# Attention values of all four head pairs projected in one token-major series ahead of the pair loop

## The chip, the cores and the metric

One core of a Trainium2 chip. The metric is the device time of one execution in microseconds (us), as the median of several runs.

## What is computed

Two transformer-like blocks over 512 tokens of width 1024, all in float32. The change touches the first block's attention: `z = rms_norm(x) @ w_in` is split into q, k, v (512 columns each, 8 heads of 64) and zu, zv (512 each, for a gating branch).

```python
q, k, v, zu, zv = jnp.split(z, [D_ATTN, 2*D_ATTN, 3*D_ATTN, 3*D_ATTN + D_SGU], axis=-1)
q = q.reshape(B, S, N_ATTN_HEADS, HEAD_DIM) * (HEAD_DIM ** -0.5)
attn = dilated_attention(q, k, v, rel_bias)
sgu = spatial_gating(jax.nn.gelu(zu), jax.nn.gelu(zv), sgu_ln_g, sgu_ln_b, sgu_w, sgu_b)
mix = jnp.concatenate([attn, sgu], axis=-1) @ w_out
```

The rest (output projection, feed-forward, and a second block of convolution, pooling, a recurrence and gated feed-forwards) is the same in both kernels.

## The kernel before, in words

Activations lie channel-major: partitions are channels, the free axis is the 512 tokens. Each float32 factor is split into a high and a low part; a product of two is three matmuls (low weights x high activations, high x low, high x high) added in PSUM. Weights come in *units* of two tiles of 128x512: SyncE loads `raw` (a ring of `RING` = 4 units), ScalarE rounds it to `whi` (`split`, two units ahead of use), GpSimd makes `wlo = raw - whi` (`lo_parts`), and TensorE waits for `unit_lo`. `unit_begun` counts units that TensorE has begun, and frees ring slots for `split`. PSUM has 8 banks of 128x512; `bank_plan` writes out by hand which stage uses which bank, and the counters `filled` and `drained` hand them over. Every engine has its own program, in the order in which the code is written.

The start: x is transposed and normalised; the zv projection goes by tokens (`unit_by_tokens`: the activations are the stationary operand, so the result has tokens on partitions) into banks 0 to 3. Then TensorE transposes the convolution taps and the eight gate weights (`small`), and projects pair 0 (`group(U_QKV, 0, "qkv0", up_tags)`): 4 units, 96 matmuls, into bank 0 (q), 1 (k), 2 (v), 3 (u = zu). A unit holds two k-tiles of the columns of all four outputs of one pair. Then come the gate's mixes and the pair loop. `PAIRS` = 4, two heads each.

`attend(p)` on TensorE: the value product of the pair before (`values`, L2221), the transposes of this pair's values (`values_turned`, L2212), and then eight weight tiles i, each a score product (`scores`, L2204 and L2205, bank 4 or 5), a bias and maximum on VectorE (`biased`), an exponential on ScalarE (`weights`, L1280), a scaling on VectorE (`scaled_weights`, L2919 and L2922) and four transposes (`turn`, L2240, bank 6 or 7) that ScalarE copies out (`turned`, L1286). Between them stand pieces of the next pair's projection (`dense`, L2000), cut by a table; one piece is three matmuls:

```python
def attend(p, piece, before_it, following=None,
           cuts=(0, 2, 4, 6, 8, 10, 12, 14, 16, 18, 20, 22, 24, 28, 30, 31, 32)):
```

The last pair has pieces of the output projection instead, under its own table `(0, 2, 4, 5, 7, 8, 10, 11, 13, 14, 15, 16, 17, 20, 21, 24)`. Scores 0 and 1 of the next pair come at the end of a pair; they need q and k as high parts (`drain_head`, ScalarE) and low parts (`qk_low`, VectorE). ScalarE also copies v out of bank 2 (`drain_values`) and the turned values into `vtok` (`values_copied`). Pairs 1 and 2 are a hardware loop on TensorE and ScalarE, pairs 0 and 3 are written out. VectorE's program is written out for all.

Of the kernel before, what the change touches and what calls it, by code (L numbers as in the profile page):

```python
# [23 lines left out]
P = 128  # L24
SEQ = 512
# [47 lines left out]
U_QKV = U_ZV + 4  # L73
U_WOUT = U_QKV + 4 * PAIRS
# [161 lines left out]
def bank_plan():  # L236
# [43 lines left out]
def build(nc, x, w, vec, sgu_w, sgu_b, rel_bias, dw_w, pool_w, ident_c, onehot_c, lnmult_c,  # L280
# [4 lines left out]
    with ExitStack() as ctx:  # L285
# [35 lines left out]
        with ExitStack() as s:  # L321
            first_table = sb("first_table", [P, PHASES * SHIFTS, P], scope=s)
            below_pdiff = sb("below_pdiff", [P, 12 * SEQ - PHASES * SHIFTS * P], scope=s)
            pdiff = sb("pdiff", [P, 4, SEQ], scope=s)
        m_hi = sb("m_hi", [P, KT, SEQ], F32R)
# [9 lines left out]
        with ExitStack() as s:  # L335
# [10 lines left out]
            vT = rs  # L346
# [9 lines left out]
            vtok = sb("vtok", [P, SEQ], scope=s)  # L356

# [258 lines left out]

        def own_rows(e):

            return slice(HEAD_DIM * e, HEAD_DIM * (e + 1))
# [103 lines left out]
        def _(sp):  # L723
# [45 lines left out]
            qkv(0, (0, 1))  # L769
# [9 lines left out]
            qkv(0, (2, 3))  # L779
# [6 lines left out]
            for p in range(1, PAIRS):  # L786
                qkv(p, range(4))
                bias_table(p)
# [326 lines left out]
        def _(act):  # L1115
# [124 lines left out]
            split(U_QKV, 0)  # L1240
# [4 lines left out]
            split(U_QKV, 1)  # L1245
# [17 lines left out]
            def drain_values(stage, turn):  # L1263
                act.wait_ge(filled[2], nth(stage, ("m", 2), turn))
                act.activation(vT[:, :], bank(stage, ("m", 2)), ACT.Copy).then_inc(drained[2], 1)

            drain_head("qkv0", 0, 0, 0)
            drain_head("qkv0", 0, 0, 1)
            drain_values("qkv0", 0)
            split(U_QKV, 3)  # L1270
# [5 lines left out]
            def attend(p, u_count, units, before_it, following=None):  # L1276
# [12 lines left out]
                def values_copied():  # L1289
                    act.wait_ge(filled[6], nth("att", "vtok", p))  # L1290
                    act.activation(vtok[:, :], bank("att", "vtok"), ACT.Copy).then_inc(drained[6], 1)

# [14 lines left out]
                if following is None:  # L1307
                    weights(1)
                    values_copied()
# [21 lines left out]
                values_copied()  # L1331
# [20 lines left out]
                units(3)  # L1352
# [4 lines left out]
                drain_values("qkv", following)  # L1357

            u_first = nth("qkv0", ("m", 3))
            attend(0, u_first, lambda i: split(U_QKV + 4, i), None, 0)  # L1360
            with act.Fori(0, PAIRS - 2) as r:
                attend(r + 1, r + (u_first + 1), lambda i: split(U_QKV + 8, i, r, 4), r, r + 1)
# [617 lines left out]
        def _(pe):  # L1980
# [184 lines left out]
            for j in range(1, 4):  # L2165
                unit_by_tokens(j)

            pe.wait_ge(small_in, 16 * 2)
            pe.wait_ge(drained[5], before("small", "taps"))
            pe.transpose(bank("small", "taps")[:, 0:4 * TAPS], trows[:, :], ident[0:4 * TAPS, 0:4 * TAPS])\  # L2170
                .then_inc(filled[5], 1)
            for i in range(2):
                pe.wait_ge(drained[4 + i], before("small", f"ws{i}"))
                for g in range(4):
                    mm = pe.transpose(ps[:, 4 + i, g * P:(g + 1) * P], wsin[:, 4 * i + g, :], ident[:, :])
                mm.then_inc(filled[4 + i], 1)

            group(U_QKV, 0, "qkv0", up_tags)
# [28 lines left out]
            def values_turned(p):  # L2207

                pe.wait_ge(drained[2], nth("qkv0", ("m", 2)) + p)
                pe.wait_ge(drained[6], before("att", "vtok", p))  # L2210
                for t in range(TT):
                    mm = pe.transpose(ps[:, 6, t * P:(t + 1) * P], vT[:, t * P:(t + 1) * P], ident[:, :])  # L2212
                mm.then_inc(filled[6], 1)

            def values(p):

                pe.wait_ge(drained[6], nth("att", ("t", 6), p))
                pe.wait_ge(drained[7], before("att", "o", p))
                for k in range(TT):
                    for e in range(2):  # L2220
                        mm = pe.matmul(ps[own_rows(e), 7, :], vtok[:, k * P + HEAD_DIM * e:k * P + HEAD_DIM * (e + 1)],  # L2221
                                       probT[:, e, k, :], start=k == 0, stop=k == TT - 1)
                mm.then_inc(filled[7], 1)

            def attend(p, piece, before_it, following=None,
                       cuts=(0, 2, 4, 6, 8, 10, 12, 14, 16, 18, 20, 22, 24, 28, 30, 31, 32)):

                def dense(n):
                    lo, hi = cuts[n], cuts[n + 1]
                    for j in range(4):  # L2230
# [14 lines left out]
                values_turned(p)  # L2245
# [16 lines left out]

            def head_units(j0, j, part, turn=0, per=0):
                behind_mixes = j0 == 4 and j == 0
                unit(U_QKV + j0, j, h_hi, h_lo, (2 * j, 2 * j + 1), "qkv", up_tags, j == 0, j == 3, turn, per,
                     (2, 0, 1, 3) if behind_mixes else (0, 1, 2, 3), use=turn + (j0 // 4 - 1), part=part)
# [21 lines left out]
            attend(0, lambda j, part: head_units(4, j, part), None, 1)  # L2288
            with pe.Fori(0, PAIRS - 2) as r:
                attend(r + 1, lambda j, part: head_units(8, j, part, r, 4), r, r + 2)  # L2290
# [387 lines left out]
        def _(dve):  # L2678
# [153 lines left out]
            for b in (5, 6):  # L2832
# [3 lines left out]
            dve.wait_ge(filled[5], nth("small", "taps"))  # L2836
            dve.tensor_copy(taps[:, 0:TAPS, :], bank("small", "taps")[:, 0:4 * TAPS].rearrange("p (t j) -> p t j", j=4))\
                .then_inc(drained[5], 1)
            for i in range(2):
                dve.wait_ge(filled[4 + i], nth("small", f"ws{i}"))  # L2840
                dve.tensor_copy(wsT[:, 4 * i:4 * i + 4, :], bank("small", f"ws{i}").rearrange("p (g t) -> p g t", t=P))\
                    .then_inc(drained[4 + i], 1)


# [9 lines left out]
            for t in range(TT):  # L2854
                dve.wait_ge(drained[t], nth("zv", ("t", t)))
                dve.tensor_scalar(zneg[:, t:t + 1], zsum[:, t:t + 1], -1.0 / (4 * P), None, ALU.mult).then_inc(zmean_ready, 1)
            for e in range(2):
# [1117 lines left out]
```

## Time and profile before

| | us |
|---|---|
| median of 3 runs | 1688.95 (1688.62 to 1689.82) |
| the profiled execution | 1689.87 |
| its span, first to last instruction | 1687.8 |
| TensorE busy in it | 1679.1 |
| VectorE, ScalarE, GpSimd busy | 1242.8, 810.6, 424.0 |

The span is what the rows lie in; the execution's time is 2.1 us more. A busy TensorE is not TensorE at its peak, since matmul ends are modelled; the start times of its rows are what to compute with.

### The profile page before, as it was taken

Reading aid. Unit: us, or ns where it says so; the run is one execution under the profiler, and the core shown is the slowest. Engines: PE = TensorE matmul, PEld = TensorE weight load, DVE = VectorE, ACT = ScalarE, POOL = GpSimd, SP = SyncE. Lnnn points to the kernel's source line nnn. Section 1 sums busy time; section 2 is a strip of 40 time slices with the busy share of each in tenths; the row PEclk is TensorE's granted clock in tenths of the full one; section 3 lists DMA queues with packets and bytes.
Section 4 is the critical chain, followed back from the end, with each engine's and each line's share of the span. In section 5 each row is a group of like instructions: output and inputs, shape, how many; then the busy total and the mean of one; then the engine's idle time right before and its main releaser. Section 6 shows DMA issues by size and latency. Waiting matters only on the chain.

```text
span 1687.8 us, 29256 instructions
## 1 busy us (share of the span) xinstructions
PE 1679.1 (99%) x9774; PEld 1468.6 (87%) x9774; DVE 1242.8 (74%) x2276; ACT 810.6 (48%) x1429; POOL 424.0 (25%) x217
## 2 busy tenths in 40 slices
PE   9999999999999999999999999999999999999998
PEld 7877788999998888889999998888888889999997
DVE  5656579888887878688688686576675598688685
ACT  5566563333332534754353354565655554343354
POOL 3332320000001497320220213432523310220221
PEclk9999999999999999999999999999999999999999
DMA  7542223333333233233332333231222233332331
GB/s 210 123 107 79 75 74 101 95 106 100 99 99 99 81 114 104 72 100 108 105 120 81 102 109 101 82 94 50 87 62 76 65 112 111 101 124 75 100 113 50
DMA packets 160146, 163.16 MB, mean 97 GB/s; under 512 B 10659, under 2 KB 126999, under 8 KB 160063
## 3 DMA queue, kind: packets, MB, share of 16 engines
q1 hardware_dynamic: 155599, 159.19, 31.1%
q10 hardware_dynamic: 4464, 2.89, 0.6%
q8 instruction: 49, 0.80, 0.2%
q14 instruction: 34, 0.28, 0.1%
HBM read 158.36 MB, written 3.67 MB: 96 GB/s over the span
## 4 chain that ended last, share of the span: by engine, by line
PE 93%; POOL 3%; DVE 1%; issue 1%; ACT 0%; DMA 0%; SPq 0%; DVEq 0%; POOLq 0%; ACTq 0%
PE ps L2000 36%; PE ps L2459 21%; PE ps L2484 10%; PE ps L2338 7%; PE ps L2363 6%; PE ps L2028 2%; PE ps L2566 1%; POOL wlo L1002 1%; PE ps L2039 1%; PE ps L2221 1%; PE ps L2240 1%; POOL wsum L1045 1%; POOL first_table L1008 0%; DMA lnmult<-const_lnmult 0%; PE ps L2204 0%
## 5 line engine op out<-in xcount | busy, mean ns | idle before, releaser
L1002 POOL TENSOR_TENSOR wlo<-raw,whi 128x1024 fp32r<-128x1024 f32 x60 | 145.2, 2436 | 588.4 <-ACT whi L1489 292.6
L2000 PE MATMUL ps<-h_hi,wlo 128*128 128x512 f32 x608 | 247.4, 407 | 0.1
L2000 PE MATMUL ps<-h_hi,whi 128*128 128x512 f32 x608 | 237.8, 391 | 0.0
L2000 PE MATMUL ps<-h_lo,whi 128*128 128x512 f32 x608 | 237.6, 391 | 0.0
L1124 ACT ACTIVATE whi<-raw 128x1024 fp32r<-128x1024 f32 x120 | 124.5, 1053 | 115.2 <-PE ps L2000 101.2
L2000 PE MATMUL ps<-m_hi,wlo 128*128 128x512 f32 x384 | 152.7, 398 | 0.3 <-POOL m_lo L1066 0.3
L2000 PE MATMUL ps<-m_hi,whi 128*128 128x512 f32 x384 | 149.7, 390 | 0.0
L2000 PE MATMUL ps<-m_lo,whi 128*128 128x512 f32 x384 | 149.7, 390 | 0.0
L2000 PEld LDWEIGHTS ps<-h_hi,whi 128*128 128x128 f32 x608 | 114.1, 188 | 25.3
L2000 PEld LDWEIGHTS ps<-h_hi,wlo 128*128 128x128 f32 x608 | 114.4, 188 | 22.2 <-issue 0.8
L2000 PEld LDWEIGHTS ps<-h_lo,whi 128*128 128x128 f32 x608 | 114.5, 188 | 20.9 <-issue 0.5
L1081 POOL TENSOR_TENSOR wlo<-raw,whi 128x512 fp32r<-128x512 f32 x30 | 43.1, 1467 | 355.3 <-ACT whi L1697 355.3
L3597 DVE TENSOR_TENSOR xT<-xT,ps 128x512 f32<-128x512 f32 x95 | 64.8, 686 | 86.1 <-PE ps L2484 56.6
L995 POOL TENSOR_TENSOR wlo<-raw,whi 128x1024 fp32r<-128x1024 f32 x36 | 87.7, 2442 | 160.9 <-ACT whi L1124 144.8
L1689 ACT ACTIVATE whi<-wsums 128x512 fp32r<-128x512 f32 x88 | 53.4, 626 | 147.9 <-DVE wsums L3465 147.9
L1102 POOL TENSOR_TENSOR wlo<-raw,whi 128x1024 fp32r<-128x1024 f32 x28 | 68.2, 2466 | 129.3 <-ACT whi L1124 129.3
L2459 PE MATMUL ps<-h_hi,wlo 128*128 128x256 f32 x352 | 99.6, 283 | 0.0
L2459 PE MATMUL ps<-h_lo,whi 128*128 128x256 f32 x352 | 99.6, 283 | 0.0
L2459 PE MATMUL ps<-h_hi,whi 128*128 128x256 f32 x352 | 99.6, 283 | 0.0
L2000 PEld LDWEIGHTS ps<-m_hi,wlo 128*128 128x128 f32 x384 | 72.1, 188 | 16.2 <-issue 1.5
L2000 PEld LDWEIGHTS ps<-m_hi,whi 128*128 128x128 f32 x384 | 72.1, 188 | 15.3
L2000 PEld LDWEIGHTS ps<-m_lo,whi 128*128 128x128 f32 x384 | 72.2, 188 | 14.8 <-issue 0.7
(506 smaller groups left out, 4931.6 us busy)
## 6 DMA issues: line engine op xcount, KB each, us to landing
raw<-in_ffn_w SPq DMA_DIRECT2D x264, 256.0 KB, 2.9
raw<-in_w_ff SPq DMA_DIRECT2D x128, 256.0 KB, 2.9
raw<-in_hg_w_in SPq DMA_DIRECT2D x64, 256.0 KB, 3.1
raw<-in_w_in SPq DMA_DIRECT2D x40, 256.0 KB, 4.8
raw<-in_cp_w_in SPq DMA_DIRECT2D x24, 256.0 KB, 2.9
raw<-in_w_out SPq DMA_DIRECT2D x16, 256.0 KB, 2.9
raw<-in_cp_w_out SPq DMA_DIRECT2D x16, 256.0 KB, 2.8
raw<-in_hg_w_out SPq DMA_DIRECT2D x16, 256.0 KB, 2.7
```

What stands on the lines that cost most here:

```text
L995: pool.tensor_tensor(wlo[:, u % RING, :, :], raw[:, u % RING, :, :], whi[:, u % RING, :, :].bitcast(F32), ALU.subtract).then_inc(unit_lo, 1)
L1002: pool.tensor_tensor(wlo[:, u % RING, :, :], raw[:, u % RING, :, :], whi[:, u % RING, :, :].bitcast(F32), ALU.subtract).then_inc(unit_lo, 1)
L1081: pool.tensor_tensor(lo_slot(s), raw[:, u % RING, d % 2, :], hi_slot(s).bitcast(F32), ALU.subtract)\
L1102: pool.tensor_tensor(wlo[:, u % RING, :, :], raw[:, u % RING, :, :], whi[:, u % RING, :, :].bitcast(F32), ALU.subtract).then_inc(unit_lo, 1)
L1124: act.activation(whi[:, u % RING, :, :], raw[:, u % RING, :, :], ACT.Copy).then_inc(unit_hi, 1)
L1689: act.activation(in_tiles(hi_slot(form_slot(layer, n))), form_source(layer, j, f), ACT.Copy)\
L2000: mm = pe.matmul(ps[:, b, :], wt[:, s, a, m * P:(m + 1) * P], xt[:, kts[a], :], start=starts and a == 0 and i == 0, stop=last)
L2338: mm = pe.matmul(ps[:, b, 0:HALF], wt[:, k * P:(k + 1) * P], xt[:, k, :], start=begins and TAGS[f] != "c11", stop=ends, skip_group_check=T ...
L2363: mm = pe.matmul(ps[:, 4 + m, :], wt[:, m * P:(m + 1) * P], xt[:, kt, :], start=kt == 0 and r == 0, stop=last)
L2459: mm = pe.matmul(ps[:, b, 0:HALF], wt[:, k * P:(k + 1) * P], xt[:, k, :], start=begins and TAGS[f] != "c11", stop=ends, skip_group_check=T ...
L2484: mm = pe.matmul(ps[:, 4 + m, :], wt[:, m * P:(m + 1) * P], xt[:, kt, :], start=kt == 0 and r == 0, stop=last)
L3597: dve.tensor_tensor(xT[:, k, :], xT[:, k, :], ps[:, 4 + m, :], ALU.add).then_inc(drained[4 + m], 1)
```

## The change

A new stage `v` of four units projects the values of all pairs ahead of pair 0, by tokens as zv is: the result is `vtok[:, p, ...]` with tokens on partitions, in banks 4 to 7, and ScalarE copies each bank out once. A pair's projection is then three units, one per output tile in the order k, q, u (`QKV_TILES = (1, 0, 3)`), each with all eight k-tiles of 128 columns. The transposes of the values, `vT`, `drain_values` and `values_copied` go. The taps and gate weights are transposed between the value units. The cuts table is shortened to 24 pieces, and pairs 1 and 2 are written out on TensorE and ScalarE.

```diff
-U_QKV = U_ZV + 4
-U_WOUT = U_QKV + 4 * PAIRS
+U_V = U_ZV + 4
+U_QKV = U_V + 4
+U_WOUT = U_QKV + 3 * PAIRS
+QKV_TILES = (1, 0, 3)
...
-    b.stage("small", [("taps", 5), ("ws0", 4), ("ws1", 5)])
-    b.stage("qkv0", up)
-    b.stage("sgu", [(("mix", j), (6, 7, 0, 1)[j]) for j in range(4)])
-    b.stage("qkv", up, PAIRS - 1)
-    b.stage("att", [("vtok", 6)] + [(("s", i), 4 + i % 2) for i in range(8)]
+    b.stage("small", [("taps", 2), ("ws0", 3), ("ws1", 2)])
+    b.stage("v", [(("t", t), 4 + t) for t in range(TT)])
+    b.stage("qkv0", [(("m", m), m) for m in QKV_TILES])
+    b.stage("sgu", [(("mix", j), (6, 7, 2, 0)[j]) for j in range(4)])
+    b.stage("qkv", [(("m", m), m) for m in QKV_TILES], PAIRS - 1)
+    b.stage("att", [(("s", i), 4 + i % 2) for i in range(8)]
...
-            def qkv(p, tiles):
-                for j in tiles:
-                    load(U_QKV, j, [wi[:, 2 * j + a, 0:4, p * P:(p + 1) * P] for a in range(2)], p, 4)
+            def v(units):
+                for j in units:
+                    load(U_V, j, [wi[:, 2 * j + a, 2, :] for a in range(2)])
+
+            def qkv(p):
+                for j, m in enumerate(QKV_TILES):
+                    load(U_QKV + 3 * p, j, [wi[:, 4 * a:4 * a + 4, m, p * P:(p + 1) * P] for a in range(2)])
...
             bias_table(0)
-            for p in range(1, PAIRS):
-                qkv(p, range(4))
-                bias_table(p)
+            for p in range(PAIRS):
+                qkv(p)
+                if p:
+                    bias_table(p)
...
+            split(U_V, 2)
+            act.preload_act_table_set(EXP_TABLES)
+            split(U_V, 3)
+            split(U_QKV, 0)
+            for t in range(TT):
+                act.wait_ge(filled[4 + t], nth("v", ("t", t)))
+                act.activation(vtok[:, :, t * P:(t + 1) * P], in_tiles(bank("v", ("t", t))), ACT.Copy)\
+                    .then_inc(drained[4 + t], 1)
+            split(U_QKV, 1)
             split(U_QKV, 2)
-            act.preload_act_table_set(EXP_TABLES)
...
+            def value_unit(j):
+
+                s = (U_V + j) % RING
+                pe.wait_ge(unit_lo, U_V + j + 1)
+                for a in range(2):
+                    k = 2 * j + a
+                    for i, (xt, wt) in enumerate(((h_hi, whi), (h_lo, whi), (h_hi, wlo))):
...
+                        for t in range(TT):
...
+                            mm = pe.matmul(ps[:, 4 + t, :], xt[:, k, t * P:(t + 1) * P], wt[:, s, a, :], start=begins, stop=ends)
...
+            def head_unit(p, j, part=slice(0, 8)):
+
+                stage, turn = ("qkv", p - 1) if p else ("qkv0", 0)
+                u, tag = U_QKV + 3 * p + j, ("m", QKV_TILES[j])
+                s, b = u % RING, banks.bank(stage, tag)
+                pe.wait_ge(unit_lo, u + 1)
+                if part.start == 0:
+                    pe.wait_ge(drained[b], before(stage, tag, turn))
+                for k in range(part.start, part.stop):
+                    cols = slice(k % 4 * P, (k % 4 + 1) * P)
+                    for i, (wt, xt) in enumerate(((wlo, h_hi), (whi, h_lo), (whi, h_hi))):
...
+                        mm = pe.matmul(ps[:, b, :], wt[:, s, k // 4, cols], xt[:, k, :], start=begins, stop=ends)
...
-            group(U_QKV, 0, "qkv0", up_tags)
+            value_unit(0)
+            taps_turned()
+            gate_weights_turned(0)
+            value_unit(1)
+            gate_weights_turned(1)
+            value_unit(2)
+            value_unit(3)
+            for j in range(3):
+                head_unit(0, j)
...
-                       cuts=(0, 2, 4, 6, 8, 10, 12, 14, 16, 18, 20, 22, 24, 28, 30, 31, 32)):
+                       cuts=(0, 2, 4, 5, 7, 8, 10, 11, 13, 14, 16, 17, 19, 21, 22, 23, 24)):
...
-                values_turned(p)
```

On VectorE, the copies of taps and gate weights move behind the four small operations on the zv means; the wait for the second gate-weight group is ahead of the gate's normalisation.

**TensorE, before turn 7.** The end of pair 0, from the transposes of tile 6 to those of tile 7 (L2240; in the change L2287; the dense matmuls are L2000 and L2216). Before:

```order
L2240 MATMUL ps<-ident,prob 128x128 x4
L2000 MATMUL ps<-h_hi,wlo 128x512
L2000 MATMUL ps<-h_lo,whi 128x512
L2000 MATMUL ps<-h_hi,whi 128x512
L2000 MATMUL ps<-h_hi,wlo 128x512
L2000 MATMUL ps<-h_lo,whi 128x512
L2000 MATMUL ps<-h_hi,whi 128x512
L2240 MATMUL ps<-ident,prob 128x128 x4
```

The same place now:

```order
L2287 MATMUL ps<-ident,prob 128x128 x4
L2216 MATMUL ps<-h_hi,wlo 128x512
L2216 MATMUL ps<-h_lo,whi 128x512
L2216 MATMUL ps<-h_hi,whi 128x512
L2287 MATMUL ps<-ident,prob 128x128 x4
```

Three dense matmuls stand between the last two groups of transposes where six stood; between turns 5 and 6 there are six where twelve were.

**ScalarE, the second half of pair 0.** From the exponential of tile 6 on (L1280, now L1294; the split is L1124, now L1136; the drains of k and q L1258 and L1261, now L1278 and L1281). Before:

```order
L1280 ACTIVATE ps,den<-sq,nmax 128x512
L1286 ACTIVATE probT<-ps 128x4x128
L1280 ACTIVATE ps,den<-sq,nmax 128x512
L1124 ACTIVATE whi<-raw 128x1024
L1258 ACTIVATE k_his<-ps 64x512
L1258 ACTIVATE q_parts<-ps 64x512
L1261 ACTIVATE k_his<-k_his 64x512
```

Now:

```order
L1294 ACTIVATE ps,den<-sq,nmax 128x512
L1300 ACTIVATE probT<-ps 128x4x128
L1294 ACTIVATE ps,den<-sq,nmax 128x512
L1278 ACTIVATE k_his<-ps 64x512
L1278 ACTIVATE q_parts<-ps 64x512
L1281 ACTIVATE k_his<-k_his 64x512
```

One split is gone; the two others, and everything else up to the exponential of tile 7, keep their places.

## Rows read from the trace of the kernel before

**Rows 1.** The page: TensorE's busy time, its granted clock in 40 slices.
```profile
PE 1679.1 (99%) x9774; PEld 1468.6 (87%) x9774; DVE 1242.8 (74%) x2276; ACT 810.6 (48%) x1429; POOL 424.0 (25%) x217
...
PEclk9999999999999999999999999999999999999999
```

**Rows 2.** The chain of waits, end of pair 1: start us, us, what.
```profile
122.45 2.76 PE ps L2000 x12
125.21 0.44 PE ps L2240 x4
125.65 1.39 PE ps L2000 x6
...
129.81 3.58 PE ps L2221 x16
```

**Rows 3.** Busy time of the transposes' line by stretch: pairs 0 and 1, span first.
```profile
66.09:99.71 33.62, 4.79 (x32) 3.99 (x32) 1.00 0.45 107
99.71:133.32 33.61, 4.79 (x32) 3.98 (x32) 1.00 0.37 96
```

**Rows 4.** Timeline of TensorE, projection of pair 0: start us, us, operation.
```profile
37.95 1.20 PE L2175 MATMUL ps<-ident,wsin 128*128 128x128 f32 x8
39.22 0.47 PE L2000 MATMUL ps<-h_hi,wlo 128*128 128x512 f32 x1
39.53 0.39 PE L2000 MATMUL ps<-h_lo,whi 128*128 128x512 f32 x1
...
60.84 0.39 PE L2000 MATMUL ps<-h_hi,whi 128*128 128x512 f32 x1
```

**Rows 5.** Timeline of TensorE around value transposes and the last value product.
```profile
133.32 0.66 PE L2212 MATMUL ps<-ident,rs 128*128 128x128 f32 x4
133.73 0.48 PE L2000 MATMUL ps<-h_hi,wlo 128*128 128x512 f32 x1
...
190.68 3.65 PE L2221 MATMUL ps<-probT,vtok 128*64 128x512 f32 x16
194.26 0.50 PE L2000 MATMUL ps<-m_hi,wlo 128*128 128x512 f32 x1
```

**Rows 6.** Timeline of GpSimd, low parts of units 4 and 5.
```profile
35.13 4.73 POOL L995 TENSOR_TENSOR wlo<-raw,whi 128x1024 fp32r<-128x1024 f32 x2 [5.83 <-ACT whi L1124]
```

**Rows 7.** Timeline of TensorE: turns 0 and 4 of pair 1, turn 7 of pair 3.
```profile
103.45 0.60 PE L2240 MATMUL ps<-ident,prob 128*128 128x128 f32 x4
...
118.17 0.60 PE L2240 MATMUL ps<-ident,prob 128*128 128x128 f32 x4
...
187.69 0.40 PE L2000 MATMUL ps<-m_hi,whi 128*128 128x512 f32 x1
188.02 0.66 PE L2240 MATMUL ps<-ident,prob 128*128 128x128 f32 x4
```

**Rows 8.** Timeline of ScalarE: split and exponential in pair 1, exponential 7 of pair 3.
```profile
119.30 1.05 ACT L1124 ACTIVATE whi<-raw 128x1024 fp32r<-128x1024 f32 x1
120.25 0.69 ACT L1280 ACTIVATE ps<-sq,nmax 128x512 f32<-128x512 f32 x1
...
186.16 0.69 ACT L1280 ACTIVATE ps<-sq,nmax 128x512 f32<-128x512 f32 x1 [0.38 <-DVE nmax L2937]
```

**Rows 9.** Timeline of VectorE: the gate's normalisation, then operations of pairs 1 and 3.
```profile
50.28 4.87 DVE L2867 SCALAR_TENSOR_TENSOR sgu_vt<-gv,zstat,ln_rows 128x512 f32<-128x512 f32 x4
...
107.08 0.75 DVE L2922 TENSOR_SCALAR prob<-ps,rden 128x512 f32<-128x512 f32 x1
...
121.96 0.68 DVE L2934 CUSTOM_DVE_ANT_0 sq<-ps,btab 128x512 f32<-128x512 f32 x1
...
126.59 0.68 DVE L2878 SCALAR_TENSOR_TENSOR q_parts<-ps,q_parts 64x512 fp32r<-64x512 f32 x1
...
185.25 0.68 DVE L2934 CUSTOM_DVE_ANT_0 sq<-ps,btab 128x512 f32<-128x512 f32 x1
...
187.21 0.75 DVE L2922 TENSOR_SCALAR prob<-ps,rden 128x512 f32<-128x512 f32 x1
```

More of the change, by code:

```diff
@@ L324, in build @@
             pdiff = sb("pdiff", [P, 4, SEQ], scope=s)
+        with ExitStack() as s:
+            below_vtok = sb("below_vtok", [P, KT, SEQ], scope=s)
+            vtok = sb("vtok", [P, PAIRS, SEQ], scope=s)
         m_hi = sb("m_hi", [P, KT, SEQ], F32R)
@@ L1244, in _ @@
                     .then_inc(sgu_sq, 1)
-            split(U_QKV, 1)
+            split(U_V, 1)
             act.wait_ge(sgu_sq, TT)
@@ new lines, in taps_turned, with gate_weights_turned @@
+            def taps_turned():
+                pe.wait_ge(small_in, 16 * 2)
+                pe.wait_ge(drained[2], before("small", "taps"))
+                pe.transpose(bank("small", "taps")[:, 0:4 * TAPS], trows[:, :], ident[0:4 * TAPS, 0:4 * TAPS])\
+                    .then_inc(filled[2], 1)
+            def gate_weights_turned(i):
+                b = banks.bank("small", f"ws{i}")
+                pe.wait_ge(drained[b], before("small", f"ws{i}"))
+                for g in range(4):
+                    mm = pe.transpose(ps[:, b, g * P:(g + 1) * P], wsin[:, 4 * i + g, :], ident[:, :])
+                mm.then_inc(filled[b], 1)
@@ L2205, in scores @@
                 pe.matmul(ps[:, b, :], q_parts[:, e, cols], k_his[:, e, :], start=False, stop=True).then_inc(filled[b], 1)
[L2207 to L2213, printed above, removed]
             def values(p):
+                if p == 0:
+                    for t in range(TT):
+                        pe.wait_ge(drained[4 + t], nth("v", ("t", t)))
                 pe.wait_ge(drained[6], nth("att", ("t", 6), p))
@@ L2220, in values @@
                     for e in range(2):
[L2221 to L2222 removed]
+                        mm = pe.matmul(ps[own_rows(e), 7, :], value_rows(p, k, e), probT[:, e, k, :], start=k == 0,
+                                       stop=k == TT - 1)
                 mm.then_inc(filled[7], 1)
             def attend(p, piece, before_it, following=None,
[L2226 removed]
+                       cuts=(0, 2, 4, 5, 7, 8, 10, 11, 13, 14, 16, 17, 19, 21, 22, 23, 24)):
                 def dense(n):
                     lo, hi = cuts[n], cuts[n + 1]
[L2230 removed]
+                    for j in range(3):
                         part = slice(max(lo - 8 * j, 0), min(hi - 8 * j, 8))
@@ L2261, in attend @@
                     scores(1, following)
[L2263 to L2266, printed above, removed]
             order = ((4, 5), (0, 1), (6, 7), (2, 3))
@@ L2287, in _ @@
             mixes((2, 3))
-            attend(0, lambda j, part: head_units(4, j, part), None, 1)
-            with pe.Fori(0, PAIRS - 2) as r:
-                attend(r + 1, lambda j, part: head_units(8, j, part, r, 4), r, r + 2)
+            attend(0, lambda j, part: head_unit(1, j, part), None, 1)
+            for p in range(1, PAIRS - 1):
+                attend(p, lambda j, part: head_unit(p + 1, j, part), p - 1, p + 1)
             attend(PAIRS - 1, wout_early, PAIRS - 2, None, (0, 2, 4, 5, 7, 8, 10, 11, 13, 14, 15, 16, 17, 20, 21, 24))
@@ L2856, in _ @@
                 dve.tensor_scalar(zneg[:, t:t + 1], zsum[:, t:t + 1], -1.0 / (4 * P), None, ALU.mult).then_inc(zmean_ready, 1)
+            dve.wait_ge(filled[2], nth("small", "taps"))
+            dve.tensor_copy(taps[:, 0:TAPS, :], bank("small", "taps")[:, 0:4 * TAPS].rearrange("p (t j) -> p t j", j=4))\
+                .then_inc(drained[2], 1)
+            for i in range(2):
+                b = banks.bank("small", f"ws{i}")
+                dve.wait_ge(filled[b], nth("small", f"ws{i}"))
+                dve.tensor_copy(wsT[:, 4 * i:4 * i + 4, :], bank("small", f"ws{i}").rearrange("p (g t) -> p g t", t=P))\
+                    .then_inc(drained[b], 1)
             for e in range(2):
```

55 lines of the change are left out of this document (20 added, 35 removed).

## The prediction

> **What bounds the kernel now.** The page comes first. TensorE is busy 1679.1 of 1687.8 us at a granted clock of 9 tenths or more in every slice [rows 1]: nothing can be gained that does not take work, or a wait, off TensorE. The change lies in the first 200 us, so I read there the chain of waits, the busy time by stretch and the timelines of three engines. In the chain through a pair [rows 2] TensorE follows TensorE: six dense matmuls take 1.39 us (0.232 each), twelve 2.76, four transposes 0.44. The pairs take 33.62 and 33.61 us, TensorE busy throughout [rows 3]. Between projection and pairs it doesn't stop either: from 39.53 to 60.84 us lie 94 matmuls, 0.2267 us each [rows 4]. So two things decide: TensorE's work, and whether ScalarE and VectorE, which make the softmax between the score matmuls and the transposes, still keep ahead when a pair gets shorter.
>
> **Work that stays.** Before, each pair's projection is 4 units of 24 matmuls, 384 for four pairs. Now there are 4 value units of 24 ahead and 3 units of 24 per pair: 96 + 288 = 384. They are all 128x512, so no matmul is saved. 24 of them move out of each of the three pairs that carry a projection, 72 in all, into the stretch ahead.
>
> **Removed: the transposes of the values.** Four per pair. Before, the dense work starts 0.41 us after the first of them (133.32 to 133.73); where dense work follows the value product directly it starts 3.58 us after the product's start (190.68 to 194.26) [rows 5], the same 3.58 that the product takes ahead of transposes [rows 2], so nothing is lost at the new border. 4 x 0.41 = **-1.64 us**. ScalarE's two copies per pair (values out, vtok in) go too; they ran beside TensorE and are worth nothing by themselves.
>
> **Moved: 72 matmuls.** In the pairs a group of six costs 1.39 us [rows 2], so 24 are 5.56 and 72 are -16.68 us; ahead of the pairs 72 cost 72 x 0.2267 = +16.32 [rows 4]. Net **-0.36 us**. The value units have the form of the zv projection (activations stationary); I take the same pace for them.
>
> **The start of that stretch.** Before, eight transposes take from 37.95 to 39.22 us [rows 4]; at 0.11 each (0.44 for four [rows 2]) they need 0.9, and the rest is a bank that ScalarE empties late. Value units write banks 4 to 7, which are free. **-0.3 us**; bounds 0 and -0.4. The first value unit wants its low part at 37.84 instead of 39.2; GpSimd begins the two of 4.73 us at 35.13 [rows 6], so the first lands about 37.5: 0.3 us to spare, which is the thinnest cover here. If it is gone, its lateness adds directly. Its weights now lie in rows of 512 elements instead of four pieces of 128, which makes that load no slower.
>
> VectorE now waits for the second group of gate weights until TensorE has done two value units (37.9 + 48 x 0.2267 + transposes, about 49.9 us, where that was 39), and behind that wait stand the gate's normalisations, which ended at 55.2 [rows 9]; 11 us later is 66. The mixes that need them come after 168 matmuls, at about 77. ScalarE's four copies of the values begin when the last value unit ends, near 61, and the q and k drains follow at 66 and later: all covered. On SyncE, pair 0's loads now come behind bias table 0, where those of pair 1 stood; same unit numbers, same queue position, and the ring holds four units with each lasting 5.4 us.
>
> **Now the pair, where the cover goes.** A pair would be 33.61 - 0.41 - 5.56 = 27.64 us if nobody waited. Its steps shrink from 3.68 us (transposes 0.44, scores 0.46, twice six matmuls at 1.39) to 2.99, as one group of six becomes three (0.70). The last pair has that step already, and TensorE waits there once, 0.1 us before the last transposes (0.33 from 187.69 to 188.02 where 0.23 is usual) [rows 7]. But in the last pair ScalarE has no q/k to drain and no weight split in its first half. I lay the two rows of work side by side three times. "Turn i" are the transposes of weight tile i.
>
> *Scores 4.* From turn 0 (103.45) to VectorE's scaling of tile 2 (107.08) are 3.63 us, with a split and the tanh in front of the exponential; from a scaling's start to TensorE's start behind it are 0.81 (187.21 to 188.02): 4.44 [rows 7, 9]. These do not shrink with the pair. TensorE wants the bank at turn 1 (2.99) + 0.44 + 0.70 = 4.13. **Wait 0.31.** Before, it came at 3.68 + 0.44 + 1.39 = 5.51.
>
> *Turn 7.* From turn 4: exponential 6 starts 2.08 us later (118.17 to 120.25 has the same copy and split in front), the next bias-and-maximum 1.71 after that (120.25 to 121.96), exponential 7 0.91 after that (185.25 to 186.16), and TensorE can start turn 7 1.86 later (186.16 to 188.02): 6.56 [rows 7 to 9]. TensorE arrives at 2.99 + (0.44 + 1.39) + (0.44 + 0.70) = 5.96, where before 12 and 6 matmuls stood between these turns. **Wait 0.60.**
>
> *Scores 0 of the next pair.* The scaling starts 0.81 us before turn 7 and keeps VectorE 0.67; then come the low parts of k and q, 0.72 and 0.68 [rows 9], and 0.06 to hand over: 1.32 after turn 7 starts; TensorE comes at 0.44 + 0.70 = 1.14. **Wait 0.18.**
>
> Then the value product (3.58 us) gives both engines room again, so nothing carries over. 1.09 us per pair, three pairs: **+3.3 us**. No such wait has a row before. Its lower bound is 0; the upper is twice the sum, 6.6, if every handoff costs 0.2 to 0.3 more, which no row excludes. I take the sum of rows.
>
> **The loop is written out.** Two of the four pairs were a loop on TensorE and ScalarE. Pair 0, outside it, takes 33.62 and pair 1, inside, 33.61 [rows 3]: no gain. The Trainium skill (Runtime: NRT & Kernel Launch, Instruction fetch mechanics) says that a taken branch out of the fetch window stalls the engine and favours unrolling; by it the sum would be lower by some unknown part, but the two periods leave it 0.01 us.
>
> **Sum.** -1.64 - 0.36 - 0.3 + 3.3 = +1.0 us. Against the profiled execution's 1689.87 that is 1690.9; the median of the runs is 0.92 lower, so I predict **1690.0 us**. After the pairs TensorE runs dense as before and the rest just shifts.
>
> **Rivals.**
> 1. *The waits don't come* (my distances hold slack the engines can use, since TensorE's queue absorbs them). For it: in the last pair six steps of 2.3 to 3 us cost one wait of 0.1. Against: that pair lacks the drains and early split. Time: 1688.95 - 2.3 = 1686.6. Chance 0.15.
> 2. *The softmax loop between ScalarE and VectorE becomes the bound.* From one exponential to the next it can't go faster than 1.71 + 0.91 = 2.62 us, and with a split of 0.95 (119.30 to 120.25) in it 3.6 [rows 8, 9], over the 2.99 of a step. It decides once a step's late handoff is not made up in the next. Then each of six steps in three pairs waits some 0.3 instead of three places: 5.4 - 2.3 = +3.1 at least, with the boundary waits +5.5: 1692 to 1694.5, say 1694. For it: two splits in steps 3 and 4. Against: only one step in three has one, and bank double-buffering lets a tile take two steps. Chance 0.12.
> 3. *TensorE loses its clock in the pairs.* Before, no slice shows less than full clock [rows 1], and its one wait in the pairs is 0.1; now gaps of 0.6 appear. The price for one pair at half the granted clock is its own length again, +28 us: 1718. The Trainium skill (TensorE: Matmul & The Clock Gate, A second HAM failure mode) says that short idle times between groups can make the clock oscillate; it speaks against this change. In the trace the clock stayed full over that one wait; no run here shows it over longer ones. Chance 0.01.
> 4. *Faster by more than expected*: no waits and the matmuls in the pairs at 0.2267 instead of 0.232 (some 270 of them, -1.4): 1685.2. Chance 0.04.
>
> My forecast has the remaining 0.68.
>
> **How the numbers follow.** 0.2% is 3.4 us, about what a measurement tells from no change: faster means below 1685.6, slower above 1692.3. Forecast (1688.5 to 1691.8) and rival 1 lie inside; rival 4 is faster; rival 3, most of rival 2 and a tail of the forecast (a late first value unit, waits near twice) are slower: 0.04, 0.83, 0.13. The range 1686.5 to 1693.0 holds both inner cases and the lower part of rival 2.
>
> **What would show it.** After: value transposes gone; 96 matmuls of the value line at 0.2267; pairs of about 28.7 us; rows of TensorE waiting for VectorE's prob and q_parts of 0.2 to 0.6 us, three per pair; the mixes at about 77 us instead of 61; the dense run behind the last value product from about 195.3 us instead of 194.26. It is wrong if the pairs take 27.6 (rival 1), over 30 (rival 2), if TensorE waits for wlo or raw at 38 us, or if the clock row dips. If the pairs are as said and the total still differs, the difference lies behind 195 us, where I expect nothing.

## The result, and the profile after

| | before | change |
|---|---|---|
| median, us (22 runs each) | 1689.54 (1688.51 to 1690.84) | 1691.78 (1690.87 to 1693.04) |
| ratio to before, 95% interval | 1 | 1.0015 (1.0009 to 1.0021) |
| span of the profiled execution, us | 1687.8 | 1689.5 |
| mixes begin, us | 61.16 | 76.47 |
| last value product begins, us | 190.68 | 192.41 |

The change makes the kernel 2.24 us slower, 0.13% of it, with an interval that excludes equal times; it is still inside the 0.2% that I called "same". I had forecast +1.0 us. In absolute time I had said 1690.0 and the runs gave 1691.78, inside the range of 1686.5 to 1693.0; 0.59 us of the 1.78 between them is the kernel before itself, 1688.95 in the three runs that I started from and 1689.54 here.

The page of the changed kernel reads almost like that of before. Its lines on busy time and on the granted clock, which answer to [rows 1]:

```profile
span 1689.5 us, 29165 instructions
...
PE 1678.3 (99%) x9758; PEld 1464.9 (87%) x9758; DVE 1240.4 (73%) x2276; ACT 809.3 (48%) x1425; POOL 424.0 (25%) x217
...
PEclk9999999999999999999999999999999999999999
```

TensorE has 16 instructions fewer, the value transposes, and 0.8 us less of busy time; the span is 1.7 us longer. So work went and idle time came. Where it came shows in TensorE's waits from 76 to 195 us (engine, line, what it waited for: us in total, times, longest). Before, the one loss in this stretch was the 0.1 us at turn 7 of pair 3 [rows 7]:

```profile
PE ps L2287 <- DVE prob L2962: 1.3, 3, 0.4
PE ps L2256 <- DVE prob L2962: 0.7, 3, 0.2
PE ps L2256 <- issue: 0.3, 2, 0.2
```

L2287 are the transposes of the weights (turn 7), L2256 the first score matmul (scores 4, and scores 0 of the next pair, whose short wait is put down to "issue"). The periods of pairs 1 and 2, counted from value product to value product as in [rows 3] (window, span, then busy time of PE and PEld for the transposes' line, granted clock, and other columns that aren't used here):

```profile
107.14:136.31 29.17, 4.85 (x32) 3.90 (x32) 1.00 0.28 75
136.31:165.47 29.16, 4.85 (x32) 3.90 (x32) 1.00 0.17 55
```

A pair takes 29.17 us, where I had 28.7, at full clock. The chain of waits at the end of pair 1, which before ran through TensorE alone [rows 2], now runs through the softmax (start us, us, what):

```profile
127.60 1.05 ACT whi L1136
128.65 0.71 ACT ps L1294 x2
129.38 0.17 DVE rden L2959
129.58 0.75 DVE prob L2962
130.33 0.60 DVE sq L2974
130.97 0.17 DVE nmax L2977
131.16 0.82 ACT ps L1294 x2
132.01 0.17 DVE rden L2959
132.21 0.76 DVE prob L2962
...
133.01 0.66 PE ps L2287 x4
...
134.52 0.47 PE ps L2256
```

The part shown begins with a weight split (whi) on ScalarE, goes through the exponentials (L1294) and the scalings (prob), and only reaches TensorE at turn 7. A chain that enters another engine in every pair is what a new bound looks like, though TensorE is still busy 99% of the span.

The three places on TensorE's timeline in pair 1 (start us, us, line, operation, and in brackets idle time and what ended it):

```profile
117.95 0.40 PE L2216 MATMUL ps<-h_hi,whi 128*128 128x512 f32 x1
118.58 0.47 PE L2256 MATMUL ps<-k_lo,q_parts 128*128 128x512 f32 x1 [0.24 <-DVE prob L2962]
118.89 0.39 PE L2257 MATMUL ps<-k_his,q_parts 128*128 128x512 f32 x1
...
132.19 0.40 PE L2216 MATMUL ps<-h_hi,whi 128*128 128x512 f32 x1
133.01 0.66 PE L2287 MATMUL ps<-ident,prob 128*128 128x128 f32 x4 [0.43 <-DVE prob L2962]
133.43 0.48 PE L2216 MATMUL ps<-h_hi,wlo 128*128 128x512 f32 x1
...
133.97 0.40 PE L2216 MATMUL ps<-h_hi,whi 128*128 128x512 f32 x1
134.52 0.47 PE L2256 MATMUL ps<-k_lo,q_parts 128*128 128x512 f32 x1 [0.15 <-issue]
134.83 0.39 PE L2257 MATMUL ps<-k_his,q_parts 128*128 128x512 f32 x1
```

Two things in these rows matter. The bracket counts from the modelled end of the matmul before (0.40 after its start), but in a dense row the next would have started 0.23 after it. What a wait costs is the distance between starts less 0.23: at scores 4 it is 118.58 - 117.95 - 0.23 = 0.40, not the 0.24 in the bracket. And the matmul behind the waiting one follows later too: 0.31 after it instead of 0.23. Counted so, a pair loses

- at scores 4: 0.40 + 0.08 = 0.48 us
- at turn 7: (133.01 - 132.19 - 0.23) + (133.43 - 133.01 - 0.36) = 0.59 + 0.06 = 0.65 (0.36 is the usual distance from four transposes to the matmul behind them)
- at scores 0: (134.52 - 133.97 - 0.23) + 0.08 = 0.32 + 0.08 = 0.40

together 1.53 us, and 29.17 - 1.53 = 27.64: just the pair that I had worked out for the case that nobody waits.

The stretch from the first matmul behind the zv projection to the mixes was 37.84 to 61.16 before, 23.32 us. Now:

```profile
37.19 1.07 PE L2185 MATMUL ps<-whi,h_hi 128*128 128x512 f32 x4
...
76.47 0.77 PE L2240 MATMUL ps<-wsT,sgu_vt 128*64 128x128 f32 x10
...
192.41 1.08 PE L2268 MATMUL ps<-probT,vtok 128*64 128x512 f32 x4
```

That is 39.28 us, +15.96. From the mixes to the last value product were 129.52 us and are 115.94, -13.58. The sum is +2.38; the runs say +2.24. (The point at which this stretch begins differs between the profiled executions, 37.1 to 39.1 us over all kernels of this study. The changed kernel's profile began 0.65 us earlier than that of before, so the two spans differ by 1.7 only. In what follows I compare the time from mixes to last value product, which is free of that.) Behind the last value product nothing changed: from its start to the end of the span are 1497.1 us in both kernels.

### The profile page after: what moved, and what is told of

It reads as the page before. It is cut to its first block, busy times and chain, and to the rows that moved or that the text cites. A ratio compares the mean times of both kernels' runs of the same rounds, so it can differ in the third digit from the quotient of the medians.

```text
span 1689.5 us, 29165 instructions
## 1 busy us (share of the span) xinstructions
PE 1678.3 (99%) x9758; PEld 1464.9 (87%) x9758; DVE 1240.4 (73%) x2276; ACT 809.3 (48%) x1425; POOL 424.0 (25%) x217
## 4 chain that ended last, share of the span: by engine, by line
PE 93%; POOL 3%; ACT 1%; DVE 1%; issue 1%; DMA 0%; SPq 0%; DVEq 0%; POOLq 0%; ACTq 0%
PE ps L2006 32%; PE ps L2500 21%; PE ps L2525 10%; PE ps L2379 7%; PE ps L2404 6%; PE ps L2216 3%; PE ps L2034 2%; PE ps L2607 1%; PE ps L2185 1%; POOL wlo L1014 1%; PE ps L2045 1%; PE ps L2268 1%; POOL wsum L1057 1%; PE ps L2287 1%; POOL first_table L1020 0%
## 5 line engine op out<-in xcount | busy, mean ns | idle before, releaser
L2006 PE MATMUL ps<-h_hi,wlo 128*128 128x512 f32 x480 | 194.7, 406 | 0.0
L2006 PE MATMUL ps<-h_hi,whi 128*128 128x512 f32 x480 | 187.7, 391 | 0.0
L2006 PE MATMUL ps<-h_lo,whi 128*128 128x512 f32 x480 | 187.3, 390 | 0.0
L1136 ACT ACTIVATE whi<-raw 128x1024 fp32r<-128x1024 f32 x120 | 124.6, 1054 | 122.6 <-PE ps L2006 104.4
L2006 PEld LDWEIGHTS ps<-h_hi,whi 128*128 128x128 f32 x480 | 90.1, 188 | 19.7
L2006 PEld LDWEIGHTS ps<-h_hi,wlo 128*128 128x128 f32 x480 | 90.3, 188 | 17.6 <-issue 0.5
L2006 PEld LDWEIGHTS ps<-h_lo,whi 128*128 128x128 f32 x480 | 90.4, 188 | 16.9 <-issue 0.5
```

The source lines that it names most:

```text
L1136: act.activation(whi[:, u % RING, :, :], raw[:, u % RING, :, :], ACT.Copy).then_inc(unit_hi, 1)
L2006: mm = pe.matmul(ps[:, b, :], wt[:, s, a, m * P:(m + 1) * P], xt[:, kts[a], :], start=starts and a == 0 and i == 0, stop=last)
```

## The experiments

Medians of the runs are of 11 runs of each kernel, with the kernel before in between on the same chip (33 runs): 1689.28 us for the first four, 1689.32 for the last four. All changes are made to the changed kernel, but for the fifth. "Pairs" is the time from the mixes to the last value product; in the changed kernel it is 115.94 us and a middle pair takes 29.17.

| kernel | median, us | ratio to before (95%) | pairs, us | a middle pair |
|---|---|---|---|---|
| splits later | 1691.36 | 1.0014 (1.0004 to 1.0023) | 115.98 | 29.18 |
| one piece before turn 7 | 1689.55 | 1.0001 (0.9992 to 1.0010) | 113.95 | 28.51 |
| both | 1690.43 | 1.0007 (0.9998 to 1.0016) | 114.69 | 28.76 |
| transposes put back | 1693.18 | 1.0024 (1.0015 to 1.0033) | 117.41 | 29.59 |
| before, loop written out | 1689.39 | 1.0000 (0.9991 to 1.0009) | 129.51 | 33.61 |
| splits in idle time | 1689.10 | 0.9997 (0.9988 to 1.0006) | 112.87 | 28.17 |
| idle time and one piece | 1687.75 | 0.9991 (0.9982 to 1.0000) | 111.67 | 27.75 |
| another table of pieces alone | 1687.47 | 0.9989 (0.9980 to 0.9998) | 111.56 | 27.67 |

**Weight splits behind the exponentials.** The chain above starts with a split. If ScalarE does the three splits of a pair later than the exponentials that are wanted first, the waits at scores 4 and turn 7 should go.

```diff
                 turned(0)
-                units(0)
                 u_tangent()
                 weights(2)
+                units(0)
...
                 turned(3)
-                units(1)
                 weights(5)
+                units(1)
                 turned(4)
-                units(2)
                 weights(6)
                 turned(5)
                 weights(7)
                 drain_head("qkv", following, following + 1, 0)
+                units(2)
```

> The changed kernel with three weight splits per pair moved later on ScalarE only: behind exponential 2 (was in front of it), behind exponential 5, and behind the first drain of k and q (was in front of exponential 6). TensorE's program is untouched. Theory (the new loss is the waits at scores 4, turn 7 and scores 0, made by the splits in front of the exponentials): scores 4 and turn 7 no longer wait, scores 0 waits 0.3 to 0.4 as before; a pair takes 28.1 instead of 29.17 us, total 3.2 us less than the change, so about 1 us below the kernel before. Rival (the loss comes from elsewhere: the code written out, the stretch ahead of the pairs): the pairs keep 29.2 us and the total stays at +2.2 us over before.

Measured: 1691.36 us, pairs 115.98, nothing gained. The waits at scores 4 and turn 7 did go, but a new one came a step later, at scores 5. The chain of waits there:

```profile
118.76 2.22 DVE ug L2939
121.00 0.69 DVE ug L2942
121.80 0.76 DVE prob L2962
122.60 0.50 PE ps L2256
```

VectorE's multiplication of the gate, L2939, takes 2.2 us. All four of it in this kernel (lowest, median and highest ns; three take 2.28 or 2.29 us, the one in the last pair 0.68), beside GpSimd's low part on the timeline:

```profile
L2939 DVE SCALAR_TENSOR_TENSOR ug<-ss,ug x4: 682/2282/2291, 89.5 to 176.5; 128x512 f32<-128x512 f32 x4
```

```profile
118.01 2.41 POOL L1007 TENSOR_TENSOR wlo<-raw,whi 128x1024 fp32r<-128x1024 f32 x1 [9.55 <-ACT whi L1136]
```

The split's high part ends later, so GpSimd's subtraction (118.01 to 120.42) falls on L2939 (118.67 to 120.96) instead of ahead of it. The split moved 1.2 us against the turn ahead of it, and GpSimd with it. 2.29 us instead of 0.68 are 1.6 too many, the scaling of tile 3 comes late by the part that isn't absorbed, and TensorE stands 1.2 us from one start to the next. I had looked at ScalarE's queue alone, and not at what a later split does to GpSimd. The Trainium skill (SBUF — State Buffer, SBUF: two separate sides) says that VectorE, in an operation with two operands in SBUF, and GpSimd, in one that reads SBUF, hold a shared pair of ports by turns and the loser stands still altogether. By that rule the trace agrees: L2939 reads ss and ug, both in SBUF, and it ends 0.54 us after GpSimd does, which is most of its own 0.68: while both were there, it did next to nothing. The bias-and-maximum just ahead (L2974, 117.88 to 118.56), which reads one of its operands from PSUM, lies over the start of the same subtraction and took its usual 0.68.

**One dense piece moved ahead of turn 7.** TensorE comes too early at turn 7 by 0.6 us, and a piece of three matmuls takes 0.70. The piece is taken from behind scores 2 and put in front of turn 6. (A piece is an eighth of a weight unit; piece numbers cuts[n] to cuts[n+1] run in the n-th gap between turns and scores.)

```diff
-                       cuts=(0, 2, 4, 5, 7, 8, 10, 11, 13, 14, 16, 17, 19, 21, 22, 23, 24)):
+                       cuts=(0, 2, 3, 4, 6, 7, 9, 10, 12, 13, 15, 16, 18, 21, 22, 23, 24)):
```

> The changed kernel with one dense piece of three matmuls per pair moved from behind scores 2 to in front of turn 6; ScalarE untouched. Theory: the wait of 0.65 us at turn 7 goes, those at scores 4 (0.48) and scores 0 (0.4) stay; 2.1 us less than the change over three pairs, so equal to the kernel before within 0.3 us. Rival (the softmax between ScalarE and VectorE bounds the whole pair): the wait moves to another place and the pair stays at 29.2 us, +2.2 us over before.

Measured: 1689.55 us, pairs 113.95 (-1.99), a middle pair 0.66 shorter: what turn 7 cost, 0.65. Scores 0 keeps its gap. On the timeline of TensorE the dense matmul ahead of scores 0, and scores 0:

```profile
132.63 0.40 PE L2216 MATMUL ps<-h_hi,whi 128*128 128x512 f32 x1
...
133.14 0.47 PE L2256 MATMUL ps<-k_lo,q_parts 128*128 128x512 f32 x1
```

The score matmul still comes 0.51 after the dense one instead of 0.23. One piece covers turn 7 and next to nothing more: turn 7 now starts 0.90 us after the start of its scaling (130.83 to 131.73), where 0.80 is the least (132.21 to 133.01 in the change). The two waits hang together, though, since the scaling and the parts of k and q follow each other on VectorE: what TensorE is later at turn 7 than it must be, it has to spare at scores 0. Two runs below show that.

**Both edits.** The two diffs above together.

> Both edits at once. Theory: no wait of TensorE is left in pairs 0 to 2 but one of 0.1 us at scores 2 of pair 0; a pair takes 27.65 us (33.61 less the transposes 0.41 and 24 matmuls 5.56); 4.6 us less than the change, 2.4 us less than before. Rival (part of the loss lies outside the three waits): it stays within 1 us of before.

Measured: 1690.43 us, pairs 114.69. That is worse than the second edit by itself, since the new wait at scores 5 (1.19 between two starts) comes along. With the wait at turn 7 covered by the piece, the split's new place costs more than it gives. The waits at turn 7 and at scores 0 are both gone here: turn 7 starts 1.49 us after the start of its scaling (131.52 to 133.01), and scores 0 comes without a wait, though only one piece stands between them as before.

**The value transposes put back.** To price the term -1.64 by itself, four transposes of the values per pair are added ahead of the dense work, into a bank whose content isn't used; the values in vtok are computed as in the changed kernel.

```diff
                 if before_it is not None:
                     values(before_it)
+                else:
+                    for t in range(TT):
+                        pe.wait_ge(drained[4 + t], nth("v", ("t", t)))
+                pe.wait_ge(drained[6], before("att", ("t", 0), p))
+                for t in range(TT):
+                    pe.transpose(ps[:, 6, t * P:(t + 1) * P], vtok[:, p, t * P:(t + 1) * P], ident[:, :])
                 dense(0)
```

> The changed kernel with four unused transposes of the pair's values put back in front of each pair's dense work, on TensorE alone; no result depends on them. Theory (0.41 us of TensorE's time per pair, nothing else): 1.6 us more than the change, +3.9 us over before, the three waits per pair unchanged. Rival (the waits swallow them, since the pair is paced by ScalarE and VectorE): less than 0.5 us more.

Measured: 1693.18 us, 3.90 over the kernel before, where the change was 2.24 over it: +1.66; a middle pair 29.59 and 29.55 (+0.42, +0.39); the stretch with all four groups +1.47, which is 0.37 a group. In the timeline of TensorE:

```profile
141.09 0.66 PE L2297 MATMUL ps<-ident,vtok 128*128 128x128 f32 x4
141.50 0.48 PE L2216 MATMUL ps<-h_hi,wlo 128*128 128x512 f32 x1
```

0.41 us from the first of them to the dense work, as before the change. So the gain of removing them is real and within 0.2 us of the size I gave it. The three waits of the pair stay, since work added ahead of turn 0 delays both rows of work alike.

**The loop of the kernel before, written out.** Both loops over the two middle pairs, on TensorE and on ScalarE.

```diff
-            with act.Fori(0, PAIRS - 2) as r:
+            for r in range(PAIRS - 2):
...
-            with pe.Fori(0, PAIRS - 2) as r:
+            for r in range(PAIRS - 2):
```

> The kernel before with its loop over pairs 1 and 2 written out on TensorE and ScalarE, nothing else. Theory (the loop costs nothing, since pairs 0 and 1 took 33.62 and 33.61 us): within 0.3 us of before. Rival (a taken branch stalls the engine, or the longer code costs loading): over 0.5 us less, or more, than before.

Measured: 1689.39 beside 1689.32, ratio 1.0000; both middle pairs 33.61. The changed kernel also writes the loop out, and that part of it is worth nothing.

**Splits in ScalarE's idle time.** The other direction: ScalarE waits for TensorE ahead of a turn's copy. A split in front of that copy runs in time that was idle, and GpSimd's subtraction comes earlier, not later.

```diff
-                turned(0)
                 units(0)
+                turned(0)
...
-                turned(3)
                 units(1)
+                turned(3)
...
-                turned(4)
                 units(2)
+                turned(4)
```

> The changed kernel with each pair's three splits put in front of the copies of turns 0, 3 and 4, where ScalarE is idle, instead of behind them. TensorE untouched. The run with later splits has shown why it won nothing: GpSimd's subtraction of that unit (118.01 to 120.4) came to lie over VectorE's product for the gate, which then took 2.29 us instead of 0.68 and held up scores 5 by 0.9. Theory (splits in front of exponentials make the waits at scores 4 and turn 7, and VectorE's operations on SBUF alone stand still while GpSimd works): here GpSimd's work lies over operations on PSUM only, the gate product stays at 0.68, scores 4 and turn 7 no longer wait, scores 0 still waits 0.3 to 0.4; 3.3 us less than the change, 1 us below before. Rival (moving the splits only moves the wait): 29.2 us per pair, +2.2 us over before.

Measured: 1689.10 us, pairs 112.87 (-3.07), a middle pair 28.17 and 28.12. In the waits of TensorE from 76 to 195 us one line is left, and VectorE's L2939 is back at its length:

```profile
PE ps L2256 <- issue: 0.3, 2, 0.2
```

```profile
L2939 DVE SCALAR_TENSOR_TENSOR ug<-ss,ug x4: 682/682/684, 90.5 to 174.4; 128x512 f32<-128x512 f32 x4
```

Scores 4 and turn 7 together had cost 0.48 + 0.65 = 1.13 a pair; 29.17 - 28.15 is 1.0. Nothing but the place of three ScalarE instructions was changed, so the splits in front of the exponentials are what makes these two waits, at this distance between turns and scores. The last experiment changes the distance instead.

**Idle time and one piece.** The last wait, scores 0, goes by one piece more between turn 7 and the scores.

```diff
-                       cuts=(0, 2, 4, 5, 7, 8, 10, 11, 13, 14, 16, 17, 19, 21, 22, 23, 24)):
+                       cuts=(0, 2, 3, 4, 6, 7, 9, 10, 12, 13, 15, 16, 18, 20, 21, 23, 24)):
```

with the three splits as in the run above.

> As the run before, and one dense piece moved from behind scores 2 to behind turn 7, in front of scores 0 of the next pair. Theory: no wait of TensorE in the middle pairs, 27.65 us each, 2.3 us below the kernel before and 4.5 below the change. Rival: a wait turns up elsewhere, and it lies within 1 us of before.

Measured: 1687.75 us, pairs 111.67, both middle pairs 27.75, and no wait left in TensorE's list. The third wait had cost 0.40 a pair, and 28.15 - 27.75 is 0.40.

**Another table of pieces alone.** Can the table do all of it, with ScalarE as the change has it? Turn 0 comes one gap earlier (the gap ahead of it is empty and the two pieces stand behind it), which gives scores 4 one piece more of distance from turn 0 (five for four); and eight pieces instead of six stand between turns 4 and 7.

```diff
-                       cuts=(0, 2, 4, 5, 7, 8, 10, 11, 13, 14, 16, 17, 19, 21, 22, 23, 24)):
+                       cuts=(0, 2, 2, 4, 6, 7, 9, 10, 12, 13, 14, 16, 18, 21, 22, 23, 24)):
```

> The changed kernel with only TensorE's table of pieces altered: behind scores 2 none instead of two, one more behind turn 0, one more in front of turn 6, one from behind scores 6 to behind turn 4. ScalarE untouched, so its splits stay in front of exponentials 2, 5 and 6. Theory (each wait is a matter of how much dense work stands between a score and its transposes): scores 4, turn 7 and scores 0 no longer wait, 4.6 us less than the change and 2.3 less than before. Rival (splits on ScalarE's path bound the pair): one of the waits stays, over 1 us more than that.

Measured: 1687.47 us, pairs 111.56 (-4.38), no wait in the list. So the waits need both the splits in front of the exponentials and too little dense work between turn and scores; either can be changed. Scores 0 is cured without a piece of its own: turn 7 starts 1.29 us after the start of its scaling (129.54 to 130.83), 0.5 later than it must, and that is to spare at scores 0. The pairs by window, in the columns used above:

```profile
106.01:133.68 27.67, 4.79 (x32) 3.97 (x32) 1.00 0.30 83
133.68:161.40 27.72, 4.79 (x32) 3.98 (x32) 1.00 0.18 58
```

and the chain at the end of pair 1 is TensorE's alone again:

```profile
129.84 0.44 PE ps L2287 x4
130.28 0.71 PE ps L2216 x3
130.99 0.44 PE ps L2287 x4
131.43 0.70 PE ps L2216 x3
132.13 0.23 PE ps L2256
```

This version has the lowest median of the study: 1.85 us under the kernel before (ratio 0.9989, 0.9980 to 0.9998), and some 4 us under the change. The terms of the change without its waits are -1.64 - 0.36 - 0.3 = -2.3 us, and most of this is there once the waits are gone. Between this and the run above the intervals overlap; which of them is faster isn't told apart.

## Why the prediction was right and wrong

The sign, the places and the mechanism held; the size was off by 1.2 us of 2.24, nearly all of it in one term, the waits.

- **Value transposes, -1.64.** Right within 0.2: put back, they cost 0.42 and 0.39 in the middle pairs and 1.47 in all (1.66 by the medians of the runs).
- **72 matmuls moved, -0.36.** Right. A value unit's 24 matmuls take 5.44 us (0.2267 each), as this line of the chain of waits shows (the chain counts from the modelled end of the matmul before, 0.16 us after the start of the unit on the timeline):

```profile
37.35 5.44 PE ps L2185 x24
```

- **Start of the stretch, -0.3.** Together with the 16.32 the stretch should have grown by 16.02; it grew by 15.96. But this rests on one profile of before. In the kernel before with its loop written out, whose TensorE code here is the same, the stretch began later, at 39.12, the eight transposes took 0.96 us (39.23 to 40.19) instead of 1.27, and the stretch 23.04; against that the growth is 16.24 and the term -0.1. So the size of this term differs between executions, and one profile of before was not enough to fix it. The cover I called thinnest held: GpSimd's two low parts run from 34.19 to 38.95, the first done about 36.6, and the first value unit starts at 37.19.
- **Gate's normalisation, copies of the values, q and k drains: covered.** Right. The normalisation ends at 62.6, the mixes start at 76.47. It was even cheaper on VectorE, as these rows beside [rows 9] show:

```profile
51.24 8.67 DVE L2902 SCALAR_TENSOR_TENSOR gv<-gv,zstat,ln_rows 128x512 f32<-128x512 f32 x4
59.83 2.73 DVE L2907 SCALAR_TENSOR_TENSOR sgu_vt<-gv,zstat,ln_rows 128x512 f32<-128x512 f32 x4
```

```profile
50.69 5.20 POOL L1007 TENSOR_TENSOR wlo<-raw,whi 128x1024 fp32r<-128x1024 f32 x2 [2.29 <-ACT whi L1136]
56.24 2.45 POOL L1007 TENSOR_TENSOR wlo<-raw,whi 128x1024 fp32r<-128x1024 f32 x1 [0.35 <-ACT whi L1136]
```

  The second step took 4.87 us for four in [rows 9], 2.73 now: GpSimd is silent from 58.7 to 62.7, while before it subtracted until 52.6. The first step lies beside three of GpSimd's subtractions (50.69 to 58.69) and takes 2.17 each. It costs nothing either way, and I could have read the effect there.
- **A pair without waits, 27.64.** Right within 0.1: 29.17 - 1.53 = 27.64 in the change, 27.67 and 27.72 in the last experiment.
- **The waits, +3.3.** This step failed in its size: 1.53 a pair instead of 1.09, three pairs +4.6. The places and the order of size were right (turn 7 0.65 for 0.60, scores 4 0.48 for 0.31, scores 0 0.40 for 0.18). Turn 7 was worked out from a hand-over to transposes, and fits. The two score waits were priced with that same hand-over, and these two score matmuls started later behind VectorE than that. These rows of VectorE's timeline, beside TensorE's above, show it:

```profile
117.69 0.75 DVE L2962 TENSOR_SCALAR prob<-ps,rden 128x512 f32<-128x512 f32 x1
...
133.58 0.69 DVE L2918 SCALAR_TENSOR_TENSOR q_parts<-ps,q_parts 64x512 fp32r<-64x512 f32 x1
```

  From turn 0 (114.06) to the scaling (117.69) are 3.63 us, exactly as I had it. But from the scaling's start to scores 4 (118.58) are 0.89 where I took 0.81, and from the q part's start to scores 0 (134.52) 0.94 where I took 0.74. On top of each comes 0.08 for the second matmul, which I had left out. Twice 0.08 and 0.08 + 0.20 are 0.44 a pair: 1.53 - 1.09. (By place the difference is 0.17, 0.05 and 0.22: the matmul behind turn 7 comes 0.06 late too, and what is lost there is not lost again at scores 0.) The prediction had named the cause as the reason for the upper bound ("if every handoff costs 0.2 to 0.3 more") and then took no part of it. The remainder of the gap to the runs is 2.24 - (1.0 + 1.3) = -0.1.
- **Rival 1, no waits.** Wrong here, but it is what the kernel becomes with another table of pieces: my price was 2.3 us under the kernel before, the run 1.85 under it.
- **Rival 2, the softmax as the bound of every step.** Wrong: TensorE waits at three places, not six. The first experiment shows how near it is, since one slow VectorE operation moved the wait one step on.
- **Rival 3, the clock.** Wrong: granted clock 1.00 in each window of a pair with three waits. By the Trainium skill (TensorE: Matmul & The Clock Gate, A second HAM failure mode) short idle times between groups of matmuls can make the clock oscillate; the trace doesn't bear it out for three gaps of 0.5 to 0.8 us between starts in each pair of 29 us.
- **The written-out loop, 0.** Right: ratio 1.0000.

What stays open: why these score matmuls start later behind a wait than the transposes. It is not the instruction alone. In the run with the later splits the same score matmul, released by the same scaling, started 0.05 us behind its end (121.80 + 0.75 to 122.60), after a gap of 1.20 us between starts; behind gaps of 0.51 to 0.63 it came 0.14 to 0.27 late. The transposes were 0.05 or 0.06 late behind a gap of 0.82 and behind one of 0.33 [rows 7, 9] alike. No run varies one of these by itself.

The missing part of the hand-over could have been found before. In the pairs of the kernel before no score matmul waits, but behind them a matmul waits for VectorE's sum of squares, and VectorE's and TensorE's timelines of before have the two:

```profile
221.10 0.69 DVE L2703 TENSOR_TENSOR ss<-ss,ps 128x512 f32<-128x512 f32 x1
...
221.94 0.67 PE L2077 MATMUL ps<-ss,ones 128*128 128x256 f32 x2 [0.18 <-DVE ss L2703]
```

That is 0.15 us from VectorE's end to TensorE's start. With it in place of the transposes' 0.06, the wait at scores 4 comes out as the 0.40 that was measured from start to start.

## What to carry to other kernels

When a change takes work off the engine that bounds the kernel, lay the shortened row of its work beside the row of the engines that feed it: the distances that don't shrink (here 3.63 us from a turn to a scaling) name the places of the new waits beforehand, and then the fixed work can be regrouped to cover them, which here turned +2.2 us into -1.9. Price such a wait from start to start, with the slower first matmul behind it, and from a hand-over of the same kind of instruction behind a gap of about the same length, looked for in the whole trace and not only in the stretch that changes; where there is none, put part of the upper bound into the sum. And before an instruction is moved on one engine, follow what it releases on the others: a split moved by 1.2 us on ScalarE set GpSimd against VectorE and cost all it had saved.

## What the runs showed of the hardware

- A VectorE operation with two SBUF operands took 2.29 us instead of 0.68 when a GpSimd subtraction of 2.41 us (128x1024) ran beside it: not slowed by a share, but standing for nearly the whole of it. GpSimd lost nothing (2.39 us with this operation out of its way). A VectorE operation of the same size with one operand in PSUM kept its 0.68 us over the start of the same subtraction.
- After a wait, four transposes start 0.05 us behind the end of VectorE's scaling (132.21 + 0.75 to 133.01), the score matmul 0.14 (117.69 + 0.75 to 118.58) and, behind the q part, 0.25 (133.58 + 0.69 to 134.52). After a longer gap, of 1.20 us, the score matmul too starts 0.05 behind the scaling (121.80 + 0.75 to 122.60).
- The matmul behind a waiting one comes late too: 0.31 us after it instead of 0.23 for the score matmuls, 0.42 instead of 0.36 behind four transposes.
